# Sample attention of a hybrid decoder step: cached pages gathered in 2 KB pieces, later adaLN weight chunks loaded in four DMAs

## What is computed

```python
def adaln(c, w_ada, b_ada):
    mod = jax.nn.silu(c) @ w_ada + b_ada          # w_ada: 1024 x 6144, f32
    return jnp.split(mod[:, None, :], 6, axis=-1)

def gather_past(pool, page_table, new_rows):
    b = page_table.shape[0]
    old = pool[page_table].reshape(b, -1, N_KV_HEADS, HEAD_DIM)
    return jnp.concatenate([old, new_rows], axis=1)
...
    ksb = to_blocks(gather_past(cache_k_slc[l], page_table, ks))
    vsb = to_blocks(gather_past(cache_v_slc[l], page_table, vs))
...
    # in nsa_attend, for the selected blocks
    s = jnp.einsum('bkgqd,bkqmd->bkgqm', qh, k_sel).astype(jnp.float32) * scale
    p_slc = masked_softmax(s, (pos_sel <= q_pos[:, None])[:, :, None])
    o_slc = jnp.einsum('bkgqm,bkqmd->bkgqd', p_slc.astype(v_sel.dtype), v_sel)
```

## Time and profile before

| | |
|---|---|
| time, median of 3 runs | 906.45 us (904.29 to 907.99) |
| profiled execution, span (the only time it has) | 917.5 us |
| mean granted TensorE clock | 0.974 |
| TensorE matmuls / VectorE / ScalarE / GpSimd busy | 93% / 68% / 41% / 33% |
| bytes moved by DMA | 138.88 MB |

### The profile page before, as it was taken

The page is one execution under the profiler, slowest core; times in us unless marked ns, Lnnn a source line. Parts: engine busy times, 40 slices in busy tenths (PEclk is TensorE's granted clock), DMA queues, the critical chain, the costliest instruction groups (busy, mean ns, idle before and its releaser), DMA issues.

```text
span 917.5 us, 17109 instructions
## 1 busy us (share of the span) xinstructions
PE 851.0 (93%) x6685; PEld 725.8 (79%) x6685; DVE 624.0 (68%) x1220; ACT 374.3 (41%) x754; POOL 307.3 (33%) x303
## 2 busy tenths in 40 slices
PE   3499999999997789999999998999999999999998
PEld 2366778899994456776777798999999999888886
DVE  2146686388948674668485899988888888434444
ACT  1033262132135434866833664444444446323221
POOL 6456500000003311634400328766677773000000
PEclk9699999999998887999999999999999999999999
DMA  7988922237187987393102554333333324422201
GB/s 207 323 293 320 321 79 75 92 111 262 45 299 259 351 337 275 87 303 108 36 0 92 152 139 123 92 94 92 92 94 93 93 92 165 145 92 93 74 1 52
DMA packets 89167, 138.88 MB, mean 151 GB/s; under 512 B 9268, under 2 KB 59988, under 8 KB 84799
## 3 DMA queue, kind: packets, MB, share of 16 engines
q1 hardware_dynamic: 74866, 96.26, 32.6%
q0 software_dynamic: 9376, 40.31, 12.7%
q10 hardware_dynamic: 4844, 1.21, 0.6%
HBM read 130.58 MB, written 11.31 MB: 155 GB/s over the span
## 4 chain that ended last, share of the span: by engine, by line
PE 74%; DVE 10%; issue 8%; ACT 4%; POOL 2%; another core or an unknown queue 1%; DVEq 0%; POOLq 0%; ACTq 0%
PE bank L2445 17%; PE bank L2447 17%; PE bank L2446 16%; PE bank L2513 4%; PE bank L2439 4%; PE bank L2801 2%; PE bank L2474 2%; PE bank L2714 2%; PE bank L2933 2%; PE bank L2454 2%; PE bank L2455 2%; PE bank L2965 2%; PE bank L2771 1%; DVE ring_lo L535 1%
## 5 line engine op out<-in xcount | busy, mean ns | idle before, releaser
L2445 PE MATMUL bank<-s,ring_hi 128*128 128x288 f32 x620 | 184.1, 297 | 4.5 <-DVE ring_lo L535 4.5
L2446 PE MATMUL bank<-s,ring_lo 128*128 128x288 f32 x620 | 182.9, 295 | 0.0
L2447 PE MATMUL bank<-s,ring_hi 128*128 128x288 f32 x620 | 182.3, 294 | 0.0
L2445 PEld LDWEIGHTS bank<-s,ring_hi 128*128 128x128 f32 x620 | 116.2, 187 | 5.4 <-DVE ring_lo L535 5.3
L2447 PEld LDWEIGHTS bank<-s,ring_hi 128*128 128x128 f32 x620 | 116.8, 188 | 0.0
L2446 PEld LDWEIGHTS bank<-s,ring_lo 128*128 128x128 f32 x620 | 116.4, 188 | 0.0
L535 DVE TENSOR_TENSOR ring_lo<-mem,ring_hi 128x512 fp32r<-128x512 f32 x84 | 106.6, 1304 | 2.1 <-POOL mem L987 1.8
L535 DVE TENSOR_TENSOR dn_w<-wring,dn_w 128x2048 fp32r<-128x2048 f32 (+1 forms) x11 | 23.1, 2097 | 65.8 <-ACT dn_w L532 65.8
L2445 PE MATMUL bank<-dn_w,dn_hi 128*128 128x512 f32 x160 | 62.2, 389 | 0.0
L2446 PE MATMUL bank<-dn_w,dn_lo 128*128 128x512 f32 x160 | 62.2, 389 | 0.0
L2447 PE MATMUL bank<-dn_w,dn_hi 128*128 128x512 f32 x160 | 62.2, 389 | 0.0
(11 more groups left out here) (448 smaller groups left out, 2127.4 us busy)
## 6 DMA issues: line engine op xcount, KB each, us to landing
wring<-in_w_gu SPq DMA_DIRECT2D x44, 512.0 KB
wring<-in_w_ada SPq DMA_DIRECT2D x16, 1024.0 KB
wring<-in_w_in SPq DMA_DIRECT2D x10, 1024.0 KB
wring<-in_w_down SPq DMA_DIRECT2D x10, 1024.0 KB
wring<-in_w_ada SPq DMA_DIRECT2D x16, 512.0 KB
proj<-in_x_prompt SPq DMA_DIRECT2D x4, 512.0 KB
mem<-in_state_k_win POOLq DMA_DIRECT2D x8, 256.0 KB
mem<-in_state_v_win POOLq DMA_DIRECT2D x8, 256.0 KB
```

The costliest lines, as they stand in the source:

```text
L2445: pe.matmul(dst, sh, ml, start=first and k == 0, stop=False)
L2446: pe.matmul(dst, sl, mh, start=False, stop=False)
L2447: ins = pe.matmul(dst, sh, mh, start=False, stop=last and k == len(pairs) - 1)
```

## The change

In the function `page` each slc page is now gathered in four indirect DMAs, each of 128 x 512, with four neighbouring cache rows (2 KB) to a partition. The index tile `idx` has 32 columns in place of 8, made by one VectorE instruction as before; every fourth group of 8 columns serves one of the four pieces. The wait for a slot is now for 64 counts a page, as for the `cmp` units. The chunks of the adaLN groups 1 and 2 are each loaded in four DMAs of 512 columns (2 KB to a partition), group 0 as before. What lands where, and all waits of the compute engines, are the same otherwise.

```diff
@@ constants
+    c[:, C_P8 + 2:C_P8 + 6] = 4 * (p % 8)[:, None] + np.arange(4)[None, :]
@@ decoder_kernel
-        idx = sb("idx", 8, U32)
+        idx = sb("idx", 32, U32)
@@ loads_of
-            if key[0] == "pc":
+            if key[0] == "pc" or (key[0] == "ada" and key[1]):
                 return 64
-            return 32 if key[0] == "gu" or key[:2] == ("ada", 2) or (key[0] == "wo" and key[2] == 0) else 16
+            return 32 if key[0] == "gu" or (key[0] == "wo" and key[2] == 0) else 16
@@ cache
-            eng.wait_ge(cache_loaded[slot_of(i)], 64 * (i // CR + 1) if i < 16 else 256 + 16 * (i // CR - 3))
+            eng.wait_ge(cache_loaded[slot_of(i)], 64 * (i // CR + 1))
@@ load
-                        sp.dma_start(wring[:, 2048 * (i % WR) + at0:2048 * (i % WR) + at0 + w],
-                                     a["w_ada"][0, 128 * kh:128 * kh + 128, c0:c0 + w]).then_inc(w_loaded[i % WR], 16)
-                        at0 += w
+                        piece = 512 if n else 2048
+                        for c in range(c0, c0 + w, piece):
+                            sp.dma_start(wring[:, 2048 * (i % WR) + at0:2048 * (i % WR) + at0 + piece],
+                                         a["w_ada"][0, 128 * kh:128 * kh + 128, c:c + piece]).then_inc(w_loaded[i % WR], 16)
+                            at0 += piece
@@ page
-                pool.indirect_dma_start(cring[:, slot_of(i), :], None,
-                                        a[name].rearrange("l n (c s) k d -> (l n c) (s k d)", s=16),
-                                        bass.IndirectOffsetOnAxis(idx[:, b:b + 1], 0)
-                                        ).then_inc(cache_loaded[slot_of(i)], 16)
+                for n in range(4):
+                    pool.indirect_dma_start(cring[:, slot_of(i), 512 * n:512 * n + 512], None,
+                                            a[name].rearrange("l n (c s) k d -> (l n c) (s k d)", s=4),
+                                            bass.IndirectOffsetOnAxis(idx[:, 8 * n + b:8 * n + b + 1], 0)
+                                            ).then_inc(cache_loaded[slot_of(i)], 16)
@@ the indices, on VectorE
-            frees(dve.scalar_tensor_tensor(idx[:, :], ps(("chunks",))[:, 0:NB], 8.0, cst[:, C_P8:C_P8 + 1].to_broadcast([128, NB]),
+            frees(dve.scalar_tensor_tensor(idx[:, :].rearrange("p (n b) -> p n b", n=4),
+                                           ps(("chunks",))[:, 0:NB].unsqueeze(1).to_broadcast([128, 4, NB]), 32.0,
+                                           cst[:, C_P8 + 2:C_P8 + 6].unsqueeze(2).to_broadcast([128, 4, NB]),
                                            ALU.mult, ALU.add), ("chunks",))
```

## The result

The changed kernel takes 919.97 us (median of 4, 915.85 to 923.05) and the kernel before 907.22 us beside it. That is 1.0145 times, 95% interval 1.0108 to 1.0182, or **+12.8 us**. The forecast was 912.0 us, with a range of 903 to 918. The direction was right, the size not.

A forecast was written before the change was run, and what follows sets the result against it. The sample attention was taken as bound by a loop over GpSimd gathers, DMA, VectorE transposes and TensorE, not one engine. Terms 6.9 - 2.0 - 1.0 + 1.7 = +5.6 us on 906.45 gave 912.0; own range 909 to 915, outer 903 to 918.

The forecast's parts named there:

- +6.9 us at keys(1): First term: second key page of pair 1 turned from 302.8 instead of 295.92, delaying TensorE; range 4.6 to 8.2 us.
- 3.0 won back from TensorE's stalls: Smaller packets let code fetches in sooner: 2.0 us off two stalls before values(1), 1.0 off two later ones.
- the floor of +4.6 at values(2): GpSimd's 48 issues and window loads make TensorE's third values block at least 4.6 us late, even if GpSimd never idles.
- nothing for values(3): Values of pair 3 were given no such floor, because they wait for TensorE before the issue.
- Issues 1.25 us apart: GpSimd's four gathers of a page start 1.25 us apart, so a page costs 5.0 us, not 1.3.
- TensorE idle for it at L2646: TensorE was to stand idle 6 to 7 us before this line (L2640 before the change).
- adaLN issues at no cost of their own: Forty more SyncE issues for adaLN chunks read 35 us later were priced at 0 on the path.
- a fetch stall or two gone and not all: TensorE's code stalls, 8.6 us in this stage, were expected to shrink but not all go.
- +4.7 us at values(1), where 4.9 was forecast: Delay at values(1): 6.9 at the keys less 2.0 from fetch stalls gives 4.9 us.
- The landing price: Time from the start of a page's last gather piece until VectorE may turn it: 4.0 us taken.
- the slow rival: GpSimd becomes the bound and adaLN loads slow landings to 5.2 us: up to +11.5 us, 918; chance 0.17.
- The clock term, +1.7: A new 7 us TensorE hole before the scores lowers its clock: 0 to 3.4 us, 1.7 taken.

The follow-up runs named there:

- ada_only: The kernel before with only the adaLN loads of groups 1 and 2 split into four DMAs, pages gathered whole: 909.08 us, 1.0020 of the kernel before.
- keys_only: The changed kernel with only key pages gathered in four, value pages whole: 910.49 us, 1.0012 of the kernel before.
- values_only: The changed kernel with only value pages gathered in four, key pages whole: 915.75 us, 1.0073 of the kernel before.
- ada_held: The changed kernel, SyncE holding the next adaLN loads for pairs 0 to 2 until the next pair's key pages are turned: 919.09 us, 1.0119 of the kernel before.
- gathers_only: The changed kernel with the adaLN loads as before, so only the gathers are in four: 925.48 us, 1.0209 of the kernel before.
- tiny_issues: The kernel before, whole pages, with three unread gathers of 8 bytes a partition ahead of each page: 926.90 us, 1.0230 of the kernel before.
- thin_ada: The changed kernel loading 16 of each 512 columns of the adaLN chunks of groups 1 and 2: 908.74 us, 1.0026 of the kernel before.
- before_thin: The kernel before loading one 32nd of the columns of the adaLN chunks of groups 1 and 2: 898.59 us, 0.9855 of the kernel before.
- v3_whole_again: Second run of the changed kernel with only the two value pages of pair 3 gathered whole: 965.10 us, 1.0481 of the kernel before on that chip.
- before_again: The kernel before, unchanged, profiled again on a chip where it takes about 920.7 us: 920.56 us, ratio 0.9993.
- v3_whole: The changed kernel with only the two value pages of pair 3 gathered whole: 965.04 us, 1.0473 of the kernel before on that chip.
- keys_first: The changed kernel with the keys of pair 1 issued ahead of the values of pair 0: 971.83 us, 1.0547 of the kernel before on that chip.

## Why the prediction was wrong

The prediction has one chain of delay: +6.9 us at keys(1), 3.0 won back from TensorE's stalls, at least the floor of +4.6 at values(2), and nothing for values(3). Three of its steps failed on first chips: the wait at keys(1) was longer, the wait for values landings was put at nothing, and the stalls gave nothing back. What TensorE waited for shows it (us; the first two columns as in the two rows above, the third all its waits of over 0.15 us in the 150 us behind the window issue):

| first chips | at L2646, for the keys | for values landings | all waits | time over before |
|---|---|---|---|---|
| before | 0 | 0 | 21.5 | |
| ada_only | 0 | 0 | 21.8 | +1.9 |
| keys_only | 0 | 0 | 24.2 | +2.3 |
| values_only | 4.7 | 5.8 | 27.4 | +7.5 |
| ada_held | 8.0 | 2.2 | 30.6 | +10.9 |
| after | 11.6 | 3.7 | 33.8 | +12.8 |
| gathers_only | 10.7 | 9.9 | 36.2 | +18.3 |
| tiny_issues | 14.4 | 11.4 | 40.7 | +19.7 |

The row of before is its first profile, whose start is that of the second chips; `ada_only` and `keys_only` stand for whole value pages on first chips and agree with it. `thin_ada` has 8.0, 2.1 and 26.3 where `before_thin` has 0, 0 and 16.8, and is 10.2 us longer. All waits together rise from row to row with the time, and what they have more than before is within 4 us of the time lost in every row. Most of it is in the first two columns, and both are 0 in the kernels that lose nothing that can be told. So on first chips nearly all of the loss is TensorE waiting for the key pages of pair 1 and for value pages.

**What held.** Issues 1.25 us apart, 5.0 us a page; keys(1) behind eight issues of values(0) as the first loss; TensorE idle for it at L2646; adaLN issues at no cost of their own; a fetch stall or two gone and not all; +4.7 us at values(1), where 4.9 was forecast. This last is luck in part, for values(1) scatters by 4 us between executions of kernels as fast as before.

**The first term, 6.9 us.** The page was turned +10.4 us late, and TensorE waited 11.6 where 6 to 7 was forecast. The landing price was taken at 4.0 with 5.2 as the upper bound; on the path it was 7.4, 6.4 and 7.8. I had put the adaLN loads down at 0 because their own readers are 35 us away. That they lengthen a gather that has moved into their time was only in the slow rival, and too small there. But this is the smaller part of the miss: where the landing was as forecast (`thin_ada` and `ada_held`, turned at 25.4 and 25.5), TensorE still waited 8.0 us and the loss was still 10.2 and 10.9, not 5.6.

**"For pair 3 there is no such floor: its values wait for TensorE before the issue".** That left values(3) without a price, and the reason given is the one that makes it dear: nothing of its issue can be done ahead. Released at 348.14, last piece at 356.98, used at 364.94, with TensorE idle for 3.0 us. The same holds for values(1), released by TensorE at 305.81 and used at 321.21, with 0.7 us idle. On first chips no kernel with one issue to a value page waits for these landings, and every one with four does, 2.1 to 11.4 us in all. `v3_whole_again` has the block 10.4 us earlier and saves 5.4 us, but on second chips, where nothing waits for the landing; the price of values(3) alone on a first chip was not measured.

**The floor at values(2).** +4.6 was worked out, +8.8 measured. The floor supposed a queue that never waits. GpSimd did wait, 2.90 us at 298.00 for a slot that VectorE had turned late and 1.96 at 305.81 for values(1), and its last piece left at 337.20. Yet the landing does not hold the block: in the chain TensorE comes to values(2) at 342.18 straight from the scores, without a wait. Its path there goes through the landing of values(1) at 321.21 and two stalls behind it, of 1.82 and 3.85 us.

**Fetches and clock.** -3.0 was taken for the stalls. 3.63 vanished, but 1.82, 3.85 and 2.80 stand in the chain of after, 8.5 in sum where the chain before has 8.6: no gain. The DMA records bear out that these are code fetches. In each of the three stalls one 16 KB packet of the instruction queue is moved, and TensorE goes on 1.4 to 1.5 us after its end (ends at 322.62, 329.52 and 344.77; TensorE at 324.12, 330.96 and 346.22).

The clock term, +1.7, is left open. Time at the lower level in the 120 us behind the window issue is 30.7 us before and 44.4 in after; at half speed that is up to 6.8. But `ada_only` has 44.4 as well, at a time that can't be told from before, so the extra 13.7 us need not have cost that much. At one place it shows: behind values(3) the 128 matmuls take 3.64 us, and 1.92 at 303.34.

**The base.** The sum was made on a profile whose start is that of the second chips (window issue at 277.4; `before_again` 276.2; all first-chip profiles 265 to 268) and carried over to times of first chips. The 11 us between that profile and the timed runs, which the prediction puts down to the profiler, are that start. Behind the window issue the kernels that are as fast as before agree on both (641.2 for `keys_only`, 643.2 for `before_again`), so this did not spoil the sum for first chips. For second chips it fails entirely, by a term that I had nowhere: TensorE's instructions arriving slowly while GpSimd issues. A trace of it stood in the kernel before: while GpSimd issues the two pages of values(3), `before_again` shows in its chain

```profile
350.27 0.29 issue
350.56 0.44 PE bank L2714 x6
351.00 0.29 issue
351.29 0.43 PE bank L2714 x6
```

0.73 us apart, at GpSimd's issues of 349.26 and 350.57. These two are 0.6 us together, and there are many more of them when four times as many issues lie over the scores.

**Open.** What differs between the chips, and by what way GpSimd's issues slow TensorE on two of them. How `v3_whole` and `keys_first` do on a first chip, and so how the loss there divides between values(0) and the later value pages. Why 16 extra issues cost so much less than 48 on second chips. A delay that feeds itself (late scores, late keys, issues moved over the next scores, more low clock: 68.3 us against 27.3 in the 110 us behind the window issue, up to 20 us of time) would do it, but no run shows it alone.

## What to carry to other kernels

Price a split transfer by its issues on the queue that carries it: for what stands behind it there, and for its own reader where the issue waits for that reader. There all pieces and the landing follow the wait, and "it waits for something anyway" is no cover. Take the landing price from a place with the traffic that will surround the moved transfer, not from a quiet one. When the sum has failed, list what the critical engine waited for in every variant, and see that the waits move with the times. Before a sum is carried from a profile to other times, see that the start of the span is that of the same kind of run, and measure a change to GpSimd's queue on more than one chip.

## What was not expected of the hardware

- An indirect gather costs GpSimd 1.25 us from start to start whether it moves 8 bytes, 2 KB or 8 KB a partition (`tiny_issues` costs what `gathers_only` costs). It is usable 3.8 to 4.0 us after its start where no adaLN loads run beside it (`ada_held`, and the first page of keys(1) in after), and 6.4 to 7.8 beside them.
- On two chips TensorE's weight loads and matmuls came in small batches 0.71 us apart while GpSimd issued indirect gathers. The waits of the scores' loads were 43.6 us with 64 issues in four pieces, 50.2 with 64 issues of whole pages and tiny ones, 12.9 with 32 and 6.8 with 16. On the first chips they were 5.8 to 8.7 with 64.
- The smaller packets did not keep TensorE's 16 KB code fetches from stalling it. The Trainium skill, "Runtime: NRT & Kernel Launch", section "Instruction fetch mechanics", has the crossing of a block as mostly hidden; the trace differs, with 1.82, 3.85 and 2.80 us in one stage.
